# Two edits to a hybrid encoder step: score pairs in groups of two, and a new order of splits at the last head

## The reference, cut to what matters

```python
h, gate = modulate(x, c, g_n, w_a, b_a)
xa, za, qb, kb, vb, zb, qc, kc, vc, zc, qi, ki, wi = project(h, w_i)
hs = rglru(causal_conv(xpad, cw, cb), ...)            # 8 blocks of 128 columns
ob = band_attn_prompt(qb, kb, vb, relb)               # 4 heads
oc = dsa_prompt(qc, qi, wi * N_IDX_HEADS ** -0.5, kc, vc, ki, topk)   # 4 heads
out = merge(hs, ob, oc, za, zb, zc, gbr, w_o)         # rmsnorm per branch, silu gate, w_out
```

## Time and profile before

| | before |
|---|---|
| median of 3 runs | 2434.33 us (2432.41 to 2436.16) |
| profiled execution, its own time | 2431.68 us |
| its span, first to last instruction | 2429.9 us |
| TensorE busy | 2327.0 us, 96% of the span |
| TensorE weight loads busy | 2162.6 us, 89% |
| VectorE, ScalarE, GpSimd busy | 41%, 34%, 34% |
| mean granted TensorE clock | 0.978 of full speed |

### The profile page before, as it was taken

The page is one execution under the profiler, slowest core; times in us unless marked ns, Lnnn a source line. Parts: engine busy times, 40 slices in busy tenths (PEclk is TensorE's granted clock), DMA queues, the critical chain, the costliest instruction groups (busy, mean ns, idle before and its releaser), DMA issues.

```text
span 2429.9 us, 47057 instructions
## 1 busy us (share of the span) xinstructions
PE 2327.0 (96%) x18307; PEld 2162.6 (89%) x18307; DVE 995.8 (41%) x1898; ACT 818.4 (34%) x1560; POOL 818.8 (34%) x620
## 2 busy tenths in 40 slices
PE   7799999999999999989987999999999999998997
PEld 4378899999999998979986888999999999988997
DVE  4454466663111223451128546776411123354113
ACT  2233343343333333332222333445333333333221
POOL 0232233333333333344424323343433333344441
PEclk9899999999999999989998999999999999999998
DMA  8975566664333333224423553333333333223443
GB/s 298 378 247 163 161 189 193 210 207 114 92 91 89 83 81 79 71 84 143 128 87 98 160 161 103 81 83 83 100 89 91 92 81 80 73 73 106 131 130 132
DMA packets 442882, 312.15 MB, mean 128 GB/s; under 512 B 21304, under 2 KB 413376, under 8 KB 441480
## 3 DMA queue, kind: packets, MB, share of 16 engines
q1 hardware_dynamic: 414480, 283.17, 39.9%
q10 hardware_dynamic: 28216, 26.39, 3.5%
HBM read 280.81 MB, written 30.92 MB: 128 GB/s over the span
## 4 chain that ended last, share of the span: by engine, by line
PE 90%; DVE 4%; DMA 3%; DVEq 1%; ACTq 1%; issue 0%; ACT 0%; SPq 0%
PE proj L641 24%; PE proj L643 23%; PE proj L647 23%; DMA work<-in_w_ada 3%; PE proj L710 2%; PE misc L756 2%; PE misc L917 2%; PE misc L890 2%; PE proj L741 2%; PE misc L837 1%; PE misc L899 1%; DVE act_lo L1483 1%; PE misc L594 1%; PE proj L721 1%; PE proj L567 1%; PE proj L693 1%
## 5 line engine op out<-in xcount | busy, mean ns | idle before, releaser
L641 PE MATMUL proj<-act_hi,w_hi 128*128 128x288 f32 x4288 | 1217.1, 299 | 0.0
L517 POOL TENSOR_TENSOR w_lo<-raw,w_hi 128x512 fp32r<-128x512 f32 x560 | 737.4, 1318 | 1384.6 <-ACT w_hi L1114 1323.7
L643 PE MATMUL proj<-act_lo,w_hi 128*128 128x288 f32 x4288 | 1196.0, 294 | 0.0
L647 PE MATMUL proj<-act_hi,w_lo 128*128 128x288 f32 x4288 | 912.8, 294 | 0.0
L641 PEld LDWEIGHTS proj<-act_hi,w_hi 128*128 128x128 f32 x4288 | 805.6, 188 | 37.3 <-issue 33.8
L643 PEld LDWEIGHTS proj<-act_lo,w_hi 128*128 128x128 f32 x4288 | 806.4, 188 | 2.7
L647 PEld LDWEIGHTS proj<-act_hi,w_lo 128*128 128x128 f32 x4288 | 687.0, 188 | 0.0
L1114 ACT ACTIVATE w_hi<-raw 128x512 fp32r<-128x512 f32 x536 | 337.7, 632 | 1036.2 <-PE proj L647 1023.9
L1486 DVE SCALAR_TENSOR_TENSOR acc<-work,kw_tok,acc 128x256 f32<-128x256 f32 (+3 forms) x128 | 101.3, 798 | 119.7 <-ACT work L1196 112.9
L1486 DVE SCALAR_TENSOR_TENSOR xy<-misc,hg,xy 128x512 f32<-128x512 f32 (+1 forms) x32 | 16.6, 517 | 245.0 <-PE misc L917 244.5
L1486 DVE SCALAR_TENSOR_TENSOR xy<-proj,mod,lb 128x288 f32 (+5 forms) x66 | 23.5, 412 | 177.3 <-PE proj L647 170.6
(11 more groups left out here) (230 smaller groups left out, 2315.4 us busy)
## 6 DMA issues: line engine op xcount, KB each, us to landing
raw<-in_w_in SPq DMA_DIRECT2D x448, 256.0 KB, 2.9
xy<-in_w_ada SPq DMA_DIRECT2D x64, 1024.0 KB, 7.8
work<-in_w_ada SPq DMA_DIRECT2D x32, 1024.0 KB, 10.7
raw<-in_w_out SPq DMA_DIRECT2D x128, 256.0 KB, 2.8
x_keep<-xy ACTq DMA_DIRECT2D x32, 288.0 KB, 2.6
lb<-x_keep SPq DMA_DIRECT2D x24, 288.0 KB, 3.2
x_keep<-xy ACTq DMA_DIRECT2D x4, 1152.0 KB, 8.3
out_y_prompt<-work SPq DMA_DIRECT2D x4, 1024.0 KB, 4.7
```

Source lines behind the costliest of these rows:

```text
L517: pool.tensor_tensor(w_lo[:, c, :, 0:width], raw[:, c, :, 0:width], w_hi[:, c, :, 0:width].bitcast(F32), ALU.subtract)\
L641: pe.matmul(dst, w_hi[:, c, kk, :], act_hi[:, k, cols], start=(k == 0), stop=False)
L643: pe.matmul(dst, w_hi[:, c, kk, :], act_lo[:, k, cols], start=False, stop=False)
L647: m = pe.matmul(proj[b][:, half, 0:HALF], w_lo[:, c, kk, :], act_hi[:, k, cols], start=False, stop=(k == KT - 1))
```

## The change

The order of instructions changes on TensorE, ScalarE and VectorE; no instruction is added or removed. In the score stage two chunks run together, then two score pairs together; ScalarE's and VectorE's lists are reordered to match, with VectorE's rotation ahead of adding up pairs 3 and 4. In the recurrent blocks two chunks run ahead of the gates instead of one, and late work follows the gates directly. At the last head, VectorE's subtractions for blocks 1, 3, 5, 7 stand ahead of the attention work of stage 7; ScalarE makes high parts 8 and 9 in stage 1 and 10 and 11 in stage 2 instead of all four in stage 0, and VectorE subtracts block 9 in stage 2 and block 11 in stage 3 instead of both in stage 1.

```diff
--- before.py
+++ after.py
@@ -810,16 +810,14 @@
 
                 def query_tile(q, b, use):
 
-                    chunks(QI + q, b, use, (0,))
+                    chunks(QI + q, b, use, (0, 1))
                     score(q - 2, 3)
-                    chunks(QI + q, b, use, (1,))
                     score(q - 2, 4)
                     late(q - 2, b)
                     hold(pe, late_read, LATE_AT[l] + q - 2 + l)
                     swap(QI - 1 + q, 1 - b, swap_i[:, :], qi_raw, P)
-                    chunks(QI + q, b, use, (2,))
+                    chunks(QI + q, b, use, (2, 3))
                     score(q - 1, 1)
-                    chunks(QI + q, b, use, (3,))
                     score(q - 1, 2)
 
                 query_tile(3, 0, 2)
@@ -842,20 +840,17 @@
                 def recurrent_block(g, first=False):
 
                     if first:
-                        chunks(LRU, 1, 4, (0,))
+                        chunks(LRU, 1, 4, (0, 1))
                         score(6, 3)
-                        chunks(LRU, 1, 4, (1,))
                         score(6, 4)
                         late(6, 1)
                         hold(pe, late_read, LATE_AT[l] + 6 + l)
                         swap(QI + 7, 0, swap_i[:, :], qi_raw, P)
-                        chunks(LRU, 1, 4, (2,))
+                        chunks(LRU, 1, 4, (2, 3))
                         score(7, 1)
-                        chunks(LRU, 1, 4, (3,))
                         score(7, 2)
-                        chunks(LRU + 1, 0, 5, (0,))
+                        chunks(LRU + 1, 0, 5, (0, 1))
                         score(7, 3)
-                        chunks(LRU + 1, 0, 5, (1,))
                         score(7, 4)
                         late(7, 0)
                         chunks(LRU + 1, 0, 5, (2, 3))
@@ -865,9 +860,8 @@
                         t_event(2)
                     if g == 2 and LATE[l] == AT:
                         hold(pe, late_read, LATE_AT[l] + AT + l + 1)
-                    chunks(LRU + 2 * g, 1, g + 4, (0,))
+                    chunks(LRU + 2 * g, 1, g + 4, (0, 1))
                     gates(g - 1)
-                    chunks(LRU + 2 * g, 1, g + 4, (1,))
                     late(6 + 2 * g, 1)
                     chunks(LRU + 2 * g, 1, g + 4, (2, 3))
                     chunks(LRU + 1 + 2 * g, 0, g + 5, (0, 1))
@@ -1212,14 +1206,12 @@
                 relus(1, 2)
 
                 def query_tile(q, b):
-                    upper(QI + 1 + q, (0,))
+                    upper(QI + 1 + q, (0, 1))
                     relus(q - 2, 3)
-                    upper(QI + 1 + q, (1,))
                     relus(q - 2, 4)
-                    upper(QI + 1 + q, (2,))
+                    upper(QI + 1 + q, (2, 3))
+                    take_query(q, b)
                     relus(q - 1, 1)
-                    upper(QI + 1 + q, (3,))
-                    take_query(q, b)
                     relus(q - 1, 2)
 
                 query_tile(3, 0)
@@ -1269,18 +1261,15 @@
 
                 def recurrent_block(g, first=False):
                     if first:
-                        upper(LRU + 1, (0,))
+                        upper(LRU + 1, (0, 1))
                         relus(6, 3)
-                        upper(LRU + 1, (1,))
                         relus(6, 4)
-                        upper(LRU + 1, (2,))
+                        upper(LRU + 1, (2, 3))
+                        take_input(0)
                         relus(7, 1)
-                        upper(LRU + 1, (3,))
-                        take_input(0)
                         relus(7, 2)
-                        upper(LRU + 2, (0,))
+                        upper(LRU + 2, (0, 1))
                         relus(7, 3)
-                        upper(LRU + 2, (1,))
                         relus(7, 4)
                         upper(LRU + 2, (2, 3))
                         if l == 0:
@@ -1434,8 +1423,8 @@
                         if h == 6 and s == 4:
                             root(r_b[0], 1)
                             root(r_b[1], 2)
-                        if h == 8 and s == 0:
-                            upper_y(2 * KC, 3 * KC)
+                        if h == 8 and s in (1, 2):
+                            upper_y(2 * KC + 2 * s - 2, 2 * KC + 2 * s)
                         if h == 8 and s < 7:
                             upper_out(4 + s)
 
@@ -1748,9 +1737,9 @@
                 add_scores(1, 2)
                 for q in range(2, 8):
                     take_rows(q, (q + 1) % 2)
+                    query(q, (q + 1) % 2)
                     add_scores(q - 1, 3)
                     add_scores(q - 1, 4)
-                    query(q, (q + 1) % 2)
                     add_scores(q, 1)
                     add_scores(q, 2)
                 hold(dve, evac, l * OUT + LRU + 1)
@@ -1938,11 +1927,11 @@
                             dve.drain().then_inc(roped, 1)
                         if h > 1 and s == 0:
                             head_side(h - 2, 8)
-                        if h > 0:
-                            head_side(h - 1, s)
                         if h == 7 and s == 7:
                             for j in range(1, 2 * KC, 2):
                                 lower(j, KT)
+                        if h > 0:
+                            head_side(h - 1, s)
                         if h < 8 and s == 7:
                             gate_path(t, t % 2, xy[:, G + h, :])
                             if h == 0:
@@ -1953,9 +1942,8 @@
                                 dve.drain()
                         if h == 7 and s < 6:
                             norm_branches(2 * s, 2 * s + 2)
-                        if h == 8 and s == 1:
-                            for j in range(2 * KC + 1, 3 * KC, 2):
-                                lower(j, KT)
+                        if h == 8 and s in (2, 3):
+                            lower(2 * KC + 2 * s - 3, KT)
                 head_side(7, 8)
                 invert_rms(0)
                 invert_rms(1)
```

## The result

| | before | after |
|---|---|---|
| median | 2433.37 us (4 runs, 2430.23 to 2436.16) | 2413.45 us (4 runs, 2411.3 to 2416.45) |
| profiled execution, its own time | 2431.68 us | 2413.58 us |
| its span | 2429.9 us | 2411.8 us |
| mean granted TensorE clock | 0.978 | 0.981 |

The ratio is 0.9919, with a 95% interval of 0.9905 to 0.9934: 19.9 us less, where 15.3 were forecast. 2413.45 lies inside the range.

A forecast was written before the change was run, and what follows sets the result against it. TensorE's own sequence was taken to bound the score stage, waits for VectorE and ScalarE the last head. Pairs 6.5, gates 0 and last head 8.8 sum to 15.3 us less: forecast 2419.0 us, range 2410 to 2428.5.

The forecast's parts named there:

- Score pairs: Score stage and first recurrent tile: grouping pairs two by two saves switches with projection, 6.5 us over two layers.
- the 0.54 per stretch of the forecast: Query tile, pair 1's start to late work: 13.23 us become 12.69, 0.54 less, in six stretches per layer.
- the first tile: Query tile 3: pairs 1 and 2 stood together already, only 3 and 4 are new, worth at most 0.1 us.
- Gates: Recurrent blocks: gates change places with one chunk in layer 0; taken as 0 in both layers.
- the second of its two ways: Behind layer 0's gates, late work waits out their last pass as the chunk did: 0, or 0.7 us lost.
- the 0.32 of the first way: Behind layer 0's gates, late work starts in the chunk's place at once: 0.32 us saved in each of 7 blocks, 2.2.
- Last head: Last head of both layers: moved subtractions and high parts remove TensorE's waits and some low-clock time, 8.8 us together.
- idle 0.42 and 1.98 go: TensorE's idle time ahead of the value transposes, layers 0 and 1, vanishes through VectorE's earlier subtractions: 0.42 and 1.98 us.
- 2.49 and 2.50 go: TensorE's idle time ahead of the first turn, layers 0 and 1, vanishes with high parts split behind the values' copy.
- 1.4 for the clock: Layer 1, first turn to third mix: 6.47 us against 5.05 for the same work; 1.4 us more gained.
- Part 11, the thinnest cover: VectorE's part 11 behind block 3's softmax has about 7 us; cover gone, up to 2.5 us a layer lost.
- Slower through the clock: Rival, chance 0.03: clock falls to 1.2 GHz after stretches without projection work, 21 x 1.4 = 29.4 us, giving 2448.4.

The follow-up runs named there:

- scores alone: Only the score groups' reordering (TensorE, ScalarE, VectorE), on the kernel before; 2425.97 us, ratio 0.9964.
- gates alone: Only the gates' edit, two chunks ahead of the gates instead of one, on the kernel before; 2434.11 us, ratio 0.9998.
- the last kernel: Changed kernel plus last head's keys turned ahead of the mix and three more output quarters ahead of the last branch; 2399.28 us, ratio 0.9853.
- after again: The changed kernel, unedited, measured and profiled a second time; 2414.14 us, ratio 0.9917.
- the two kernels with the three quarters: Changed kernel plus three more output quarters ahead of the last branch, 2404.51 us; the same with last head's keys turned ahead of the mix, 2399.28 us.

## Why the prediction was right, and where it was off

- **Score pairs: right, 6.84 us for 6.5.** The swap comes every 19.33 us instead of 19.87, which is the 0.54 per stretch of the forecast; six are 3.24, and 0.2 remain, where the first tile was put at 0.1. No wait came in. The Trainium skill, "TensorE: Matmul & The Clock Gate", Part 3, "The mechanism", says in its list of what overlaps that a weight load overlaps running matmuls only where row groups differ, by which the group of pairs 1 and 2 would cost as much as the two apart; its first paragraph also lets a load into "the background weight buffer" go ahead. The traces differ from the rule of the list: 1.28 us in the tile shown, 1.48 apart, and 2.08 us per layer for this group alone. The weight loads (PEld) show where the 0.2 us come from, after:

```profile
199.20 0.73 PEld L756 LDWEIGHTS misc<-ki_t,work 64*128 64x128 f32 x8 [0.17 <-issue]
...
207.00 0.30 PEld L756 LDWEIGHTS misc<-ki_t,work 64*128 64x128 f32 x4 [0.17 <-issue]
...
208.06 0.20 PEld L756 LDWEIGHTS misc<-ki_t,work 64*64 64x64 f32 x4 [0.76 <-issue]
```

  The eight loads of pairs 1 and 2 follow each other without a break that the profile marks, and by the single records the first loads of pair 2 start at 199.52, together with pair 1's last matmuls. Ahead of the four of pair 4 the loads pause for 0.76 us, and that group takes the full 1.75. Why the two groups differ was not tested.
- **Gates: right at 0**, and by the second of its two ways. Late work starts 1.07 us after the gates' last group, where the chunk started 0.76 us after it: it starts 0.31 us later behind them, and that takes back the 0.32 of the first way. No wait for weights came in: the stretch did not grow.
- **Last head: the mechanism right, the size not.** The step that failed is the sum "idle 0.42 and 1.98 go", with "2.49 and 2.50 go" and 1.4 for the clock. It priced a wait by the idle time that TensorE shows in one trace. In that trace half-clock work filled most of the first wait. Like for like, at full clock and from the tables' columns, "values" goes from 12.76 to 9.03, 3.7 us per layer where 0.42 and 1.98 were taken; "first turn" from 6.33 to 3.6, 2.7 where 2.5 was taken; "rest" stays. That is 6.4 per layer and 12.9 in all, against 8.8. The before and after traces give the same: 95.16 us from the last chunk to the third root sum in both layers together, 82.28 after. Nearly all of the error lies in the 0.42 of layer 0, where 3.7 us went: in this pair of traces layer 1 lost 2.2, 2.8 and 1.5 us, against 1.98, 2.50 and 1.4. What would have shown it in advance is the distance from the last chunk to the value transposes, 12.73 and 12.78 us although the clock differed: so the other engines set it. That the total stayed inside the range all the same is in part luck: its lower end had been drawn for the gates and the clock, not for this.
- **The 1.4 us for the clock in layer 1: right in number, not as a gain of the order.** In this pair of traces "rest" of layer 1 fell from 29.20 to 27.73, but with the old order the extra 1.4 stands now in layer 1 (before), now in layer 0 (scores alone) and now in neither (gates alone). And in the trace after, layer 1 has 1.5 us of it in "values" instead; in the second profile of that kernel layer 0 has them (9.03 and 10.57, then 10.62 and 9.04). So where it falls differs between two profiles of one order.
- **Part 11, the thinnest cover, held.** It ends at 1051.83 in layer 0, and no wait of TensorE over 0.5 us stands at the quarters behind it. The subtraction took 1.63 us while GpSimd was splitting weights; the early four took 0.76 each, quick as the forecast took them.
- **Slower through the clock** did not come: the score stage has 1.00 granted although each tile now holds 4.91 us from group 3 and 4 to the next chunk (207.00 to 211.91 by the same rows) without projection work.

The sum by the traces: 6.8 and 12.9 are 19.7, the span shrank by 18.1. The output projection of layer 1 took 2.3 us more in the trace after ("end" 182.4 to 184.7), which is the difference of pace between 130.0 and 131.7 ns per matmul that two profiles of one kernel show as well (last section).

## What to carry to other kernels

A wait's price is the distance between the two events that bound it, compared with the work in between at full clock; the idle time in one trace can be what half-clock work left over, here 0.42 us of 3.56. Where two small groups each interrupt a long stream, put them side by side: what is saved is the switch, and the trace has the price wherever two stand together already. Where half-clock work follows a wait, independent work moved into it pays more than the wait: here 6.5 us in layer 0 for waits of 4.6 (3.37 + 1.22).

## What the runs showed of the hardware that was not expected

- The same stream of 288-column matmuls, at a clock of 1.00 and without a wait, has one of three paces for a whole output projection. Busy time by stretches, the kernel before in its two layers, then the last kernel in its first:

```profile
1120.00:1220.00 100.00, 100.00 (x761) 100.00 (x761) 14.62 (x32) 25.76 (x40) 40.41 (x33) 1.00 0.44 130
2250.00:2350.00 100.00, 100.00 (x772) 100.00 (x771) 14.61 (x32) 25.82 (x40) 41.73 (x33) 1.00 0.44 132
```

```profile
1120.00:1220.00 100.00, 100.00 (x746) 100.00 (x745) 14.61 (x32) 25.09 (x39) 40.04 (x32) 1.00 0.43 128
```

  From start to start these are 131.7, 130.0 and 134.4 ns. Over the 1341 matmuls of "end" the extremes lie 6 us apart, 0.25% of the kernel, and profiles of one kernel differ in pace (after: 131.7 in both layers; after again: 130.0 in both, and a span shorter by 4.0 us). 134.4 was seen in one layer of each of the two kernels with the three quarters, and in none of the others; what sets the pace was not found.
- VectorE's subtraction of one high part took 0.76 us with GpSimd idle (from 1024.66), 1.63 us in the middle of GpSimd's splits (1050.20), and 1.84 in the old order, beside GpSimd's own four subtractions: an order of lists changes durations, not only places. It isn't always VectorE that is slowed: at 1045.26 in the trace after, it began 0.02 us ahead of a subtraction of GpSimd and took 0.76, while GpSimd's (1045.28) took 2.01 us, where the one before (1041.54) had taken 1.43. The Trainium skill, "SBUF — State Buffer", section "SBUF: two separate sides", says that when VectorE works on two inputs in SBUF and GpSimd reads SBUF, as in these subtractions, the one that starts first holds their shared port pair for its whole instruction and the other waits; the rows from 1045.26 and 1050.20 agree with it.
